# Sample value products moved by one step in a joint attention loop

## The reference, cut to what matters

```python
z = jnp.einsum('bqhd,bkhd->bhqk', q, k) * (HEAD_DIM ** -0.5) + bias
causal = k_pos[None, :] < q_pos[:, None]
log_1m_beta = jnp.where(causal, jax.nn.log_sigmoid(-z), 0.0)
tail = lax.cumsum(log_1m_beta, axis=3, reverse=True) - log_1m_beta
w = jnp.where(causal, jnp.exp(jax.nn.log_sigmoid(z) + tail), 0.0)
return jnp.einsum('bhqk,bkhd->bqhd', w, v)
```

## Time and profile before

| | us |
|---|---|
| median of 3 runs | 2962.05 |
| lowest, highest | 2961.49, 2965.26 |
| the profiled execution | 2961.77 |
| its span in the trace | 2960.3 |
| TensorE busy in it | 2712.3 |
| VectorE busy | 1345.7 |
| ScalarE busy | 961.3 |

### The profile page before, as it was taken

How to read it: one execution, slowest core, us unless ns; L and a number is a source line. 1 busy time by engine, 2 the same in 40 slices (tenths; PEclk the granted TensorE clock), 3 DMA queues, 4 the chain that set the end, 5 groups by cost and what they waited for, 6 DMA issues and landing times. The chain is left out here.

```text
span 2960.3 us, 45584 instructions
## 1 busy us (share of the span) xinstructions
PE 2712.3 (92%) x15137; PEld 1377.8 (47%) x15137; DVE 1345.7 (45%) x2726; ACT 961.3 (32%) x1858; POOL 473.7 (16%) x669
## 2 busy tenths in 40 slices
PE   7999999996789898899989999699999998899978
PEld 3444444442445454455434555355555554455533
DVE  2231414132678787788876777312212221122218
ACT  2222213021677677777761222111000100000104
POOL 0101010101021111112111222211111111111123
PEclk9999999997899999999999999799999999999989
DMA  8020111017586867676664333766986579968637
GB/s 319 15 85 15 58 42 43 15 57 291 174 277 208 275 212 257 212 246 230 224 227 144 134 128 125 268 215 220 313 283 215 180 232 358 332 218 288 224 106 312
DMA packets 275922, 575.75 MB, mean 194 GB/s; under 512 B 59270, under 2 KB 75719, under 8 KB 271740
## 3 DMA queue, kind: packets, MB, share of 16 engines
q1 hardware_dynamic: 192936, 427.99, 41.5%
q0 software_dynamic: 82480, 145.43, 15.4%
q10 hardware_dynamic: 324, 0.10, 0.0%
HBM read 460.86 MB, written 112.29 MB: 194 GB/s over the span
## 5 line engine op out<-in xcount | busy, mean ns | idle before, releaser
L1220 DVE TENSOR_TENSOR_SCAN left<-leave,left 128x512 f32<-128x512 f32 (+3 forms) x320 | 358.6, 1121 | 137.8 <-ACT leave L1102 137.0
L418 PE MATMUL bank<-xnT,w_in 128*128 128x512 f32 x768 | 330.3, 592 | 0.0
L1963 PE MATMUL bank<-w,hT 128*64 128x512 f32 x1280 | 310.7, 607 | 0.0
L1931 ACT ACTIVATE sg<-bank 128x128 f32<-128x128 f32 x160 | 44.3, 277 | 681.4 <-PE bank L1950 681.4
L1023 POOL DMA_DIRECT2D w_out<-in_cache_v x256 | 137.4, 537 | 663.9 <-issue 655.4
L1586 PE MATMUL bank<-w_out,w 128*128 128x512 f32 x512 | 229.4, 601 | 2.6 <-DVE w L1650 2.6
L1950 PE MATMUL bank<-w,o_sq 128*64 128x256 f32 x1920 | 223.7, 386 | 8.0 <-DMA w<-in_w 6.2
L418 PEld LDWEIGHTS bank<-xnT,w_in 128*128 128x128 f32 x768 | 145.6, 190 | 181.8 <-issue 180.6
L418 PE MATMUL bank<-w_in,xnT 128*128 128x512 f32 x512 | 220.4, 592 | 0.0
L1995 DVE TENSOR_TENSOR sg<-sg,bank 128x128 f32<-128x128 f32 x160 | 46.0, 288 | 373.1 <-ACT sg L1931 373.1
L1950 PE MATMUL bank<-oT,o_sq 128*64 128x256 f32 x1856 | 211.7, 381 | 1.0 <-issue 1.0
(11 more groups left out here) (383 smaller groups left out, 3308.4 us busy)
## 6 DMA issues: line engine op xcount, KB each, us to landing
w<-in_w SPq DMA_DIRECT2D x54, 2048.0 KB, 22.6
w_out<-in_cache_v POOLq DMA_DIRECT2D x256, 256.0 KB
w_out<-in_cache_k SPq DMA_DIRECT2D x256, 256.0 KB
oT<-in_w SPq DMA_DIRECT2D x22, 2048.0 KB, 19.6
w_out<-in_w SPq DMA_DIRECT2D x20, 2048.0 KB, 19.4
ys_d<-zeros SPq DMA_DIRECT2D x32, 816.0 KB
slab<-in_w_ada SPq DMA_DIRECT2D x24, 1024.0 KB, 17.5
ys_d<-y POOLq DMA_DIRECT2D x83, 256.0 KB, 9.9
```

Of the source, the lines that this page charges most:

```text
L418: mm = pe.matmul(ps[:, :], w, m, start=(i == 0), stop=(i == len(parts) - 1))
L1220: dve.tensor_tensor_scan(left[n % 4][:, 0:cols][:, ::-1], leave[n % 4][:, 0:cols][:, ::-1], leave[n % 4][:, 0:cols][:, ::-1], left[n % 4][ ...
L1963: mm = pe.matmul(yb[p * G:p * G + G, :], hT[:, half, q * G:q * G + G], w2[i][:, q * (EC // STRIPS) + half, p * XW:p * XW + XW], start=(hal ...
```

## The change

The four positions of a unit's sample value products depend on the unit's parity. The i-th product of a unit stands at the i-th position of the tuple.

```diff
--- before.py
+++ after.py
@@ -1383,8 +1383,9 @@
                         values((n - 6) // 4, (n - 6) % 4 // 2)
                     if p == 3 and u in (1, NY + 1):
                         new_values(u // NY)
-                    if p in (4, 7, 10, 13) and 1 <= u <= NU:
-                        sample_values(u - 1, (p - 4) // 3)
+                    steps = (4, 8, 10, 14) if u % 2 else (5, 7, 11, 13)
+                    if p in steps and 1 <= u <= NU:
+                        sample_values(u - 1, steps.index(p))
```

## The result

The changed kernel takes 2972.58 us in the median of 17 runs, the kernel before 2964.23 us: ratio 1.0031, 95% interval 1.0019 to 1.0044. It is slower by 8 to 9 us. The ratio leaves out one run of each kernel, of 4352.1 and 3553.1 us, far above all others; the first had a granted clock of 0.65 where the others have 0.96. The kernel before, which was at 2962.05 us in the three runs that the forecast started from, is at 2964.23 us in this longer series. The profiled execution took 2972.58 us.

The account below looks back on a forecast made before the run. It took TensorE (92% busy) to bound the kernel, VectorE close behind in the attention. Terms of -3.8, +2.3 and +1.0 us summed to -0.5 us, giving 2961.5 us, no change that can be told, range 2955 to 2968 us.

Parts of the forecast that it names:

- term 3: GpSimd's value-page loads: moved products shift later loads' requests; even units' third load about 2 us later, +1.0 us in all.
- Term 1: TensorE's own time: each product moved behind prompt values saves 0.12 us of shape change, 32 moves 3.8 us.
- third rival: TensorE tiling: both drains go, 0.21 us a move, 6.7 us in all, 2958.7 us; counted within the no-change chance of 0.69.
- Term 2: TensorE's turns after odd steps: without the product they wait for VectorE's `take`, 0 to 4.7 us, taken as +2.3 us.
- slower rival: Value pages come late at p = 13 of even units, 1.2 us a unit, +8.1 us, 2970 us; chance 0.10.
- waits of over 6 us: Sign in TensorE's waits for values: growth over 6 us, or mostly at p = 13 of even units, means late value pages.
- faster rival: Attention loop: earlier turns shorten ScalarE's and VectorE's waits, 0.15 us a move, 8.6 us less, 2953.5 us; chance 0.17.

Follow-up runs that it names:

- e7: Changed kernel, but odd units at 4, 7, 10, 14, so the fourth product's pages are requested after p = 7 again: 2962.64 us, 0.9993 to the kernel before.
- e5: Changed kernel with SyncE's zero fill behind a unit's fourth key load moved beside the other fill, behind the second: 2971.48 us, 1.0016 to the kernel before.
- e13: Changed kernel with every zero fill issued behind the attention's last load: 3190.45 us in all, attention 806.7 us.
- e3: Changed kernel with value pages loaded only for the first two products, other loads and their waits left out: 2944.30 us, 0.9933 to the kernel before.
- e4: Kernel before with value pages loaded only for the first two products, other loads and their waits left out: 2944.37 us, 0.9932.
- e6: Kernel before with SyncE's zero fill behind a unit's fourth key load moved beside the other fill, behind the second: 2962.39 us, 0.9996.
- e14: Kernel before with every zero fill issued behind the attention's last load: 3188.19 us in all, attention 798.1 us.
- e15: Changed kernel run once more, unedited, for the spread of single profiles: 2973.06 us, 1.0029 to the kernel before.
- e9: Changed kernel, but GpSimd requests value pages for the next unit's first product only when the fourth product is done: 2973.44 us, 1.0036 to the kernel before.
- e16: Odd units at 4, 7, 10, 14, even units at 5, 7, 11, 13, run once more: 2964.38 us, 1.0000 to the kernel before.

## Why the prediction was wrong

I forecast 2961.5 us and no change, with a range up to 2968; the changed kernel takes 2972.58 us and is slower by 0.31%. The step that failed is term 3, in its sentence on odd units: "In odd units the fourth load moves away from the third; its due time moves too." I priced that at nothing because the number of steps between request and due stays six. The runs show the opposite: that load is the one that costs. Its window is on average as long as before (11.4 and 11.3 us), but the request now comes behind key pages and beside and behind fills that SyncE issues for the same position, and the load lands up to 4 us too late. e7 shows the request step as the cause. e5 and e13 show the fills as what it meets in all odd units but the first. They don't show that the fills are the whole loss: without them in its way the changed order meets prompt loads in units 1, 4 and 8 and stays as far behind. I had searched SyncE's queue for what the change moves on it, and not for what the value load is moved past.

*Term 1*, the shape: right in kind and in the price of a move, too high in the number of moves. Twelve of the 32 moved pairs gain 0.10 to 0.15 us in e3 against e4; I had 0.12. The others gain next to nothing or lose, so that -1.5 us is left of the -3.8 in the sum. No pair gains the 0.21 us of the third rival. The Trainium skill (TensorEngine Tiling (Array Packing), Key Properties) says that a change of the tiling mode drains the engine. It gives no price, and the runs show the gain of a move, not a number of drains.

*Term 2*, the uncovered turn: right in kind, and where I said. Unit 12, p = 4, in the changed kernel's timeline of PE and DVE: `take` ends at 1352.37, the turn starts at 1352.43; without a wait it would start at 1351.76, so it waits 0.67 us, where I had 0.66 from the earlier trace rows.

```profile
1351.32 0.63 PE L1306 MATMUL tb<-ident,w_out 128*128 128x128 f32 x4 [0.17 <-DVE wT L1135]
1351.69 0.68 DVE L1126 TENSOR_TENSOR take<-take,left 128x512 f32<-128x512 f32 x1
1352.43 0.66 PE L1271 MATMUL tb<-ident,take 128*128 128x128 f32 x4 [0.48 <-DVE take L1126]
```

A wait that I had not listed joins it. Unit 9, p = 7: the next page turn waits 0.40 us for ScalarE's `wT` copy to free the bank, since two page turns and two turns now come close together:

```profile
1214.07 0.60 PE L1306 MATMUL tb<-ident,w_out 128*128 128x128 f32 x4
1214.50 0.60 PE L1271 MATMUL tb<-ident,take 128*128 128x128 f32 x4
1215.50 0.63 PE L1306 MATMUL tb<-ident,w_out 128*128 128x128 f32 x4 [0.40 <-ACT wT L1034]
```

Terms 1 and 2 together were -1.5 us; e3 and e4 give -0.6 us for the attention and equal times. The sum is near, but by two errors that cancel: less gained in place (1.5 us, not 3.8), and what the nine pairs lose, 3.8 us, mostly come back elsewhere (2.9 us), where I had taken half of 4.7. Two profiles of one kernel differ by more than that, so the way back is not shown.

*Term 3*, +1.0 us forecast: measured +11.6 us of waits for values in the first profile of the changed kernel and +7.8 in the second. The rest of the first attention's 14.6 us is in part the clock: 10.3 us more of it were granted at half clock than before. By the product's 1.94 us against 1.07 that is worth about half, some 5 us, as an estimate and at most. In the second profile the waits alone are about the attention's growth (6.8 us).

*The rivals.* The slower rival named the right resource and the wrong place: p = 13 of even units, where lateness stayed as it was (4.1 and 3.9 us). Its price, 1.2 us a unit and 2970 us, is close to what odd units now pay (11.1 and 7.6 us over eight units), and one of the signs I gave for it, waits of over 6 us, came. That its price fits is luck, since another load pays it for another reason. I gave it 0.10. The faster rival is out: `leave` is waited for more, not less. The third rival is out by the pairs of steps of e3 and e4; the time of e7 couldn't have told it.

*What stays open.* Why the two orders stay 9 us apart in time with the fills moved (e5 and e6), with 3.7 us between their waits for values, and why the attentions of e13 and e14 lie 8.6 us apart with 3.6 us between theirs. The lower clock is a part: 7.5 us more at half clock in e5's attention than in e6's, 17.9 in e13's than in e14's, each worth at most about half of that by the same estimate; its share wasn't isolated. How the late pages share the DMA engines with the fills, packet by packet, wasn't tried. No version beats the kernel before beyond its interval.

## What to carry to other kernels

An instruction that releases a buffer is also a request: when it moves, ask at what point of every other queue the load will now be issued, and not only whether its window keeps its length. Where both orders are run with and without the loads (e3 and e4 here), one pair of runs tells the engine's order from the transfers. And a transfer that is moved out of the way of one load can stand in the way of another: e5 cured units 5 and 9 and gained nothing. A gain of 0.12 us a step is smaller than one late transfer.

## What the runs showed of the hardware

A single wait of 4 us on TensorE was followed by more loss than its length: behind it the granted clock was 0.54 for 7 us, a product took 1.94 us instead of 1.07, and the half unit lost 6.1 us. In e15 the wait was 3.68 us and the half unit lost 4.6 us.

The stretch behind the attention, which no order of the attention touches, differs from profile to profile by more than the change does: 1412.7 us in the changed kernel, 1420.2 in its second profile (e15), 1414.7 before, 1426.0 in e9. The attention itself differs by 7.8 us between the two profiles of the changed kernel (824.1 and 816.3 us), and by as much between those of e7 and e16, which are one kernel (802.3 and 810.1 us). One execution can't tell a few us; many runs can, and waits that return at the same product in several profiles.
